# Opening the first four weight units of a two-block fp32 kernel block by block instead of one after the other

## The chip, the cores and the metric

One NeuronCore of a Trainium2 chip runs the whole program. The metric is the device time of one execution in microseconds, the median of several runs. Of the engines, PE (TensorE) multiplies, ACT (ScalarE) and DVE (VectorE) do the elementwise work, POOL (GpSimd) sets constants, and SP (SyncE) issues most transfers.

## The reference

Two transformer-like blocks on 256 tokens of width 1024, in fp32. Only the start of the first one matters here: the input is RMS-normalised and projected by one wide matrix.

```
def rmsnorm(x, g):
    xf = x.astype(jnp.float32)
    y = xf * lax.rsqrt(jnp.mean(xf * xf, axis=-1, keepdims=True) + EPS)
    return (y * g.astype(jnp.float32)).astype(x.dtype)
...
    proj = n @ w_in
    idx = np.cumsum(IN_SIZES)[:-1].tolist()
    z, xBC, dt_raw, q, k, v, r, a1, g_ssd, g_gla = jnp.split(proj, idx, axis=-1)
```

The kernel multiplies the weights with x times g and applies the factor of each token (the reciprocal root of its mean square) when the product is evacuated, so the matmuls need not wait for the norm, but every evacuation does.

## The kernel before

All big matrices come as a stream of weight **units**: 1024 inputs by 128 outputs, 512 KB, one row of 4 KB per partition. The inputs of a unit are eight **blocks** of 128. There are four slots (`RING`) in `raw`; unit u uses slot u mod 4 and PSUM bank u mod 4 of `acc`. Each fp32 operand is split into a high part, rounded to the fast matmul format, and the rest. ACT makes the high part of a unit (`split_hi`, `whi`, L1163), DVE the low part (`split_lo`, `wlo`, L1670). x times g is split the same way, block by block: `xh` on ACT (L1209), `xl` on DVE (L1677). A unit is three products per block (high by high, high by low, low by high), 24 matmuls of 128 by 256 tokens.

What sets the order is written out by hand, engine by engine, with semaphores between the engines. SP loads the next unit into a slot when `lo_ready` has counted the low part of the slot's last unit (L379 to L381). ACT may write `whi` of a slot when the slot's load has landed and PE is done with the unit that used it. PE may start a unit when its high part is there and its bank is evacuated.

The opening before: SP loads unit 0, both halves of x, unit 1, the small weights, units 2 and 3 (L367 to L373). ACT loads all the parameters (`par`), splits unit 0, the eight blocks of x, unit 1, squares x (L1212 to L1217, `sq`), splits units 2 and 3, and takes the root of the mean square (`rms`: `rt` for a row of all tokens, `rtt` for a column per token). PE runs 14 products of a constant tile as a warm-up (L713), then unit 0 block by block (L714), unit 1 (L716 to L722), the **small products** (24 matmuls with the 48 columns for dt and a gate, L592 to L600), the **statistics** (`stream_stats`, L567: the sum of the squares times 1/1024, once as a row, once per token), and from unit 2 on the ordinary `unit`. Behind unit 3 stand the **gates** (`gla_gates`, L602), which need the evacuated small products (`smt`, L1806). DVE adds the squares in four steps (L1763 to L1773), makes the reciprocals `rtok` (per token) and `rstd` (row), half of it `rstdh` (L1776), evacuates the small products, and then goes from unit to unit: evacuation (L1828), low part of the unit four further on, taps of a convolution.

Of the kernel before, what the change touches and what calls it, by code (L numbers as in the profile page):

```python
# [23 lines left out]
P = 128  # L24
F32 = mybir.dt.float32
# [9 lines left out]
KB = D // P  # L35
# [93 lines left out]
CHUNK_AT = {38: (0, 2), 40: (1, 3), 43: (4, 5)}  # L129
CONV_AT = [c + c // 2 + 1 for c in range(12)]  # L130
# [17 lines left out]
def blocks_kernel(nc, w, wsmall, wa2, par, xT, memT, metaT, out):  # L148
    with ExitStack() as ctx:
# [160 lines left out]
        def hidden(T):  # L310
# [12 lines left out]
        par_in, x_in, x2_in, meta_in, ws_in, wa_in, mem_in = [sem(n) for n in  # L323
            ("par_in", "x_in", "x2_in", "meta_in", "ws_in", "wa_in", "mem_in")]
# [148 lines left out]
        def _(pe):  # L473
# [236 lines left out]

            pe.wait_ge(consts, 2)
            for n in range(14):
                nc.tensor.matmul(mix[:, 2, 0:P], mean1024[:, :], mean1024[:, :], start=True, stop=True)  # L713
            unit("xbc", 0, 0, xh1, xl1, T1, ready=(xl_ready, 0))  # L714
            pe.wait_ge(hi_ready, 2)
            for k in range(KB):  # L716
                nc.tensor.matmul(acc[:, 1, 0:T1], whi[:, 1, k, :], xh1[:, k, 0:T1], start=k == 0, stop=False)
                nc.tensor.matmul(acc[:, 1, 0:T1], whi[:, 1, k, :], xl1[:, k, 0:T1], start=False, stop=False)
            pe.wait_ge(lo_ready, 2)
            for k in range(KB):  # L720
                last = nc.tensor.matmul(acc[:, 1, 0:T1], wlo[:, 1, k, :], xh1[:, k, 0:T1], start=False, stop=k == KB - 1)
            last.then_inc(unit_done, 1)  # L722
            small_products()
# [432 lines left out]
        def _(act):  # L1156
            def split_hi(base, units=0):

                j = base % 4
                act.wait_ge(landed[j], units * 4 + 16 * (base // 4 + 1))  # L1160
                if base >= RING:
# [1355 lines left out]
```

## Time and profile before

| | us |
|---|---|
| median of 3 runs | 1178.31 |
| lowest, highest | 1178.06, 1178.64 |
| span of the profiled execution | 1175.6 |
| PE busy in it | 1160.9 (99%) |
| DVE busy | 839.4 (71%) |
| ACT busy | 678.9 (58%) |

The span runs from the first to the last instruction of the profiled execution; some 2.7 us of the measured time lie around it. PE is busy in nine tenths or more of every slice but the first and the last. A busy PE in such a table is not a PE at its peak, since matmuls overlap; the times at which groups of matmuls begin say more than their busy time. In a timeline row the first number is the start in us from the start of the span, the second the duration of the group, "xN" the number of instructions, and the brackets tell how long the engine was idle before and what released it. A row with the engine "SPq" or "ACTq" is the issue of a transfer, and the DMA view gives the time from that start to the landing of all its data.

### The profile page before, as it was taken

What the parts mean: (1) busy time and instruction counts of PE and PEld (TensorE: products, weight loads), DVE (VectorE), ACT (ScalarE), POOL (GpSimd) and SP (SyncE); (2) the same over time, 40 slices, a digit from 0 to 9 for tenths busy, and PEclk for the clock granted to TensorE, in tenths of its full rate; (3) what the DMA queues carried; (4) which work ended last, traced back from release to release, by engine and by line L of the source; (5) the groups of instructions that cost most, each with busy time, mean ns of one, the idle gap of its engine ahead of it and who ended that gap; (6) DMA issues with size and microseconds to landing.
All of it is one profiled execution on the core that took longest, in us unless ns stands there. A gap on an engine that the chain in (4) does not pass through costs nothing.

```text
span 1175.6 us, 25261 instructions
## 1 busy us (share of the span) xinstructions
PE 1160.9 (99%) x9580; PEld 1140.0 (97%) x9580; DVE 839.4 (71%) x1249; ACT 678.9 (58%) x1029; POOL 46.6 (4%) x68
## 2 busy tenths in 40 slices
PE   8999999999999999999999999999999999999997
PEld 8999899999999999999999999999999999999997
DVE  7998767987856877776667748666545898776453
ACT  6755547656535666655556647656444777665442
POOL 2002311400000000000000000000000000000000
PEclk9999999999999999999999999999999999999998
DMA  6655434566553565656553426555565545666561
GB/s 226 190 174 175 128 107 143 183 225 187 164 159 126 164 201 190 191 185 189 180 152 113 123 73 209 176 171 190 190 180 170 160 144 165 212 182 193 182 194 54
DMA packets 56775, 197.51 MB, mean 168 GB/s; under 512 B 7153, under 2 KB 9457, under 8 KB 56577
## 3 DMA queue, kind: packets, MB, share of 16 engines
q1 hardware_dynamic: 54480, 193.68, 53.8%
q10 hardware_dynamic: 2224, 2.84, 0.8%
q8 instruction: 51, 0.84, 0.3%
q14 instruction: 20, 0.16, 0.0%
HBM read 195.45 MB, written 1.05 MB: 167 GB/s over the span
## 4 chain that ended last, share of the span: by engine, by line
PE 85%; DVE 9%; ACT 4%; issue 2%; DMA 0%; DVEq 0%; ACTq 0%
PE acc L482 14%; PE acc L483 14%; PE acc L488 14%; PE acc L476 11%; PE acc L478 11%; PE acc L477 11%; DVE wlo L1670 3%; ACT whi L1163 1%; PE acc L541 1%; PE acc L542 1%; PE acc L545 1%; PE mix L822 1%; PE mix L803 1%; DVE softp L2166 1%; DVE sp L2156 1%
## 5 line engine op out<-in xcount | busy, mean ns | idle before, releaser
L1670 DVE TENSOR_TENSOR wlo<-raw,whi 128x1024 fp32r<-128x1024 f32 x366 | 448.7, 1229 | 180.0 <-ACT whi L1163 179.8
L1163 ACT ACTIVATE whi<-raw 128x1024 fp32r<-128x1024 f32 x366 | 385.2, 1057 | 317.7 <-PE acc L488 158.5
L482 PE MATMUL acc<-xh,whi 128*128 128x256 f32 (+1 forms) x1448 | 358.2, 285 | 0.0
L483 PE MATMUL acc<-xl,whi 128*128 128x256 f32 (+1 forms) x1448 | 353.7, 282 | 0.0
L482 PEld LDWEIGHTS acc<-xh,whi 128*128 128x128 f32 x1448 | 271.8, 188 | 2.9 <-issue 2.3
L483 PEld LDWEIGHTS acc<-xl,whi 128*128 128x128 f32 x1448 | 272.7, 188 | 0.3
L488 PE MATMUL acc<-xh,wlo 128*128 128x256 f32 (+1 forms) x1448 | 202.2, 282 | 0.0
L478 PE MATMUL acc<-hh,wlo 128*128 128x256 f32 (+1 forms) x688 | 194.4, 283 | 0.0
L476 PE MATMUL acc<-hh,whi 128*128 128x256 f32 (+1 forms) x688 | 194.3, 282 | 0.0
L477 PE MATMUL acc<-hl,whi 128*128 128x256 f32 (+1 forms) x688 | 194.1, 282 | 0.0
L488 PEld LDWEIGHTS acc<-xh,wlo 128*128 128x128 f32 x1448 | 185.2, 188 | 0.0
L477 PEld LDWEIGHTS acc<-hl,whi 128*128 128x128 f32 x688 | 129.4, 188 | 0.0
L478 PEld LDWEIGHTS acc<-hh,wlo 128*128 128x128 f32 x688 | 129.3, 188 | 0.0
L476 PEld LDWEIGHTS acc<-hh,whi 128*128 128x128 f32 x688 | 129.3, 188 | 0.0
L476 PE MATMUL acc<-xh,whi 128*128 128x256 f32 (+1 forms) x272 | 77.3, 284 | 3.3 <-DVE xl L1677 3.3
L478 PE MATMUL acc<-xh,wlo 128*128 128x256 f32 (+1 forms) x272 | 76.6, 282 | 0.0
L477 PE MATMUL acc<-xl,whi 128*128 128x256 f32 (+1 forms) x272 | 76.6, 281 | 0.0
L476 PEld LDWEIGHTS acc<-xh,whi 128*128 128x128 f32 x272 | 51.1, 188 | 3.9 <-DVE wlo L1670 2.4
L482 PE MATMUL acc<-yh,whi 128*128 128x256 f32 (+1 forms) x224 | 54.3, 281 | 0.0
L483 PE MATMUL acc<-yl,whi 128*128 128x256 f32 (+1 forms) x224 | 54.3, 280 | 0.0
L477 PEld LDWEIGHTS acc<-xl,whi 128*128 128x128 f32 x272 | 51.2, 188 | 0.0
L478 PEld LDWEIGHTS acc<-xh,wlo 128*128 128x128 f32 x272 | 51.1, 188 | 0.0
(397 smaller groups left out, 1572.1 us busy)
## 6 DMA issues: line engine op xcount, KB each, us to landing
raw<-w SPq DMA_DIRECT2D x366, 512.0 KB, 3.7
hT<-xT SPq DMA_DIRECT2D x2, 512.0 KB, 6.3
mem<-memT ACTq DMA_DIRECT2D x1, 1024.0 KB, 7.3
rgw<-w ACTq DMA_DIRECT2D x2, 512.0 KB, 4.9
out<-hT SPq DMA_DIRECT2D x4, 128.0 KB, 2.5
out<-hT ACTq DMA_DIRECT2D x4, 128.0 KB, 2.8
xdt<-wsmall SPq DMA_DIRECT2D x1, 192.0 KB, 7.0
pr<-par ACTq DMA_DIRECT2D x1, 114.0 KB, 4.4
```

Source lines behind the costliest of these rows:

```text
L476: nc.tensor.matmul(dst, whi[:, slot, n, :], rh, start=first, stop=False)
L477: nc.tensor.matmul(dst, whi[:, slot, n, :], rl, start=False, stop=False)
L478: return nc.tensor.matmul(dst, wlo[:, slot, n, :], rh, start=False, stop=last)
L482: nc.tensor.matmul(dst, whi[:, slot, n, :], rh, start=first, stop=False)
L483: nc.tensor.matmul(dst, whi[:, slot, n, :], rl, start=False, stop=False)
L488: ins = nc.tensor.matmul(dst, wlo[:, slot, k, :], rh(k), start=False, stop=last and k == KB - 1)
L541: nc.tensor.matmul(dst, ah[:, k, at:at + n], whi[:, s:s + 2, k, :], start=k == 0, stop=False)
L542: nc.tensor.matmul(dst, al[:, k, at:at + n], whi[:, s:s + 2, k, :], start=False, stop=False)
L545: last = nc.tensor.matmul(dst, ah[:, k, at:at + n], wlo[:, s:s + 2, k, :], start=False, stop=k == KB - 1)
L803: last = nc.tensor.matmul(mix[:, h % 2, 256 * t:256 * t + 256], xqT[:, 2 * h + i, P * t:P * t + P], xkT[:, 2 * h + i, :], start=i == 0, st ...
L1163: act.activation(whi[:, j, :, :].rearrange("p k c -> p (k c)"), raw[:, j, :], ACT.Copy)\
L1670: dve.tensor_tensor(wlo[:, j, :, :].rearrange("p k c -> p (k c)"), raw[:, j, :], whi[:, j, :, :].rearrange("p k c -> p (k c)").bitcast(F32 ...
```

## The change

The first four units are opened together. Their weights come in five pieces by input block: blocks 0 and 1 of units 0 and 1, the same of units 2 and 3, then blocks 2-3, 4-5 and 6-7 of all four. x comes as block 0 (on ACT's queue), block 1, and then pairs, each ahead of the weights that meet it. ACT loads first only the eight parameter columns that scale x; the others go last on SP. For each piece ACT makes the high part and DVE the low part in one instruction, and PE does all products of a block for its units before it goes to the next block; only the last piece is done unit by unit. `hi_ready` and `lo_ready` jump by 4 at the last piece. The squares of blocks 0 to 3 stand behind the high part of blocks 4-5 on ACT, the others behind the last high part; the four adds stand behind the last low part on DVE. PE does the statistics before the small products, gates come behind unit 4, and the warm-up has 11 products. The row reciprocal comes first on DVE; the reciprocals per token, the halved factor and the evacuation of the small products stand behind the first evacuation and the low part of unit 4.

```diff
+LEFT = ((2, 4), (4, 6), (6, 8))
...
-            sp_.dma_start(raw[:, 0, :], w[0, :, :]).then_inc(landed[0], 16)
-            sp_.dma_start(hT[:, 0:4, META:T2], xT[:, 0:4, :]).then_inc(x_in, 16)
-            sp_.dma_start(hT[:, 4:8, META:T2], xT[:, 4:8, :]).then_inc(x2_in, 16)
-            sp_.dma_start(raw[:, 1, :], w[1, :, :]).then_inc(landed[1], 16)
+            for n in range(2):
+
+                sp_.dma_start(raw[:, 2 * n:2 * n + 2, 0:2 * P], w[2 * n:2 * n + 2, :, 0:2 * P].rearrange("j p c -> p j c"))\
+                    .then_inc(w_in[n], 16)
+                if n == 0:
+                    sp_.dma_start(hT[:, 1, META:T2], xT[:, 1, :]).then_inc(x_in[1], 16)
+            for n, (a, b) in enumerate(LEFT):
+
+                sp_.dma_start(hT[:, a:b, META:T2], xT[:, a:b, :]).then_inc(x_in[2 + n], 16)
+                sp_.dma_start(raw[:, :, P * a:P * b], w[0:RING, :, P * a:P * b].rearrange("j p c -> p j c"))\
+                    .then_inc(w_in[2 + n], 16)
             sp_.dma_start(wsr, wsmall).then_inc(ws_in, 16)
-            for j in range(2, RING):
-                sp_.dma_start(raw[:, j, :], w[j, :, :]).then_inc(landed[j], 16)
+            sp_.dma_start(pr[:, KB:NPAR], par[:, KB:NPAR]).then_inc(par_in, 16)
...
+            def open_block(units, k, n):
+
+
+                pe.wait_ge(xh_ready, k + 1)
+                pe.wait_ge(open_hi, n + 1)
+                for j in units:
+                    nc.tensor.matmul(acc[:, j, 0:T1], whi[:, j, k, :], xh1[:, k, 0:T1], start=k == 0, stop=False)
+                pe.wait_ge(xl_ready, k + 1)
+                for j in units:
+                    nc.tensor.matmul(acc[:, j, 0:T1], whi[:, j, k, :], xl1[:, k, 0:T1], start=False, stop=False)
+                pe.wait_ge(open_lo, n + 1)
+                for j in units:
+                    nc.tensor.matmul(acc[:, j, 0:T1], wlo[:, j, k, :], xh1[:, k, 0:T1], start=False, stop=False)
...
+            for n in range(2):
+                for k in range(2):
+                    open_block((2 * n, 2 * n + 1), k, n)
+            for n, (a, b) in enumerate(LEFT[:-1]):
+                for k in range(a, b):
+                    open_block(range(RING), k, n + 2)
+            pe.wait_ge(hi_ready, RING)
+            pe.wait_ge(xl_ready, KB)
+            for j in range(RING):
+                for k in range(*LEFT[-1]):
+                    high_products(acc[:, j, 0:T1], j, k, xh1[:, k, 0:T1], xl1[:, k, 0:T1], False)
+                if j == 0:
+                    pe.wait_ge(lo_ready, RING)
+                low_products(acc[:, j, 0:T1], j, range(*LEFT[-1]), lambda k: xh1[:, k, 0:T1], True)\
+                    .then_inc(unit_done, 1)
             pe.wait_ge(consts, 15)
             stream_stats("mix", T1, tiles1)
+            small_products()
...
-                    elif m > 1:
+                    elif m >= RING:
                         unit(phase, n, n % 4, xh1, xl1, T1)
-                    if m == 3:
+                    if m == 4:
                         gla_gates(0)
                         gla_gates(1)
...
+            act.dma_start(hT[:, 0, META:T2], xT[:, 0, :]).then_inc(x_in[0], 16)
+            act.dma_start(pr[:, 0:KB], par[:, 0:KB]).then_inc(mixw_in, 16)
...
+            for n in range(2):
+                act.wait_ge(x_in[n], 16)
+                block_hi(n)
+                open_hi_part(n, 2 * n, 2 * n + 2, 0, 2)
+            for n, (a, b) in enumerate(LEFT):
+                act.wait_ge(x_in[2 + n], 16)
+                for k in range(a, b):
+                    block_hi(k)
+                open_hi_part(n + 2, 0, RING, a, b)
+                if n == 1:
+                    for k in range(a):
+                        square(k, T1)
+            for k in range(4, KB):
+                square(k, T1)
...
-            inverse_rms("mix", T1, (P, P), halved=True)
-            dve.wait_ge(rstdh_ready, 1)
+            inverse_rms("mix", T1)
...
-                    if m == 0:
-
+                    if m == 1:
+
+                        for t in range(2):
+                            dve.reciprocal(rtok[:, t:t + 1], rtt[:, t:t + 1])
+                        dve.tensor_scalar(rstdh[:, 0:T1], rstd[:, 0:T1], 0.5, None, ALU.mult).then_inc(rstdh_ready, 1)
+                        dve.wait_ge(rstdh_ready, 1)
```

On ACT, the opening of the program before, from the first split of a unit (L1163; L1209 are blocks of x, L1167 squares, L1215 the small weights):

```order
L1163 ACTIVATE whi<-raw 128x1024 [waits landed0]
L1209 ACTIVATE xh<-hT,pr 128x256 [waits x_in,par_in]
L1209 ACTIVATE xh<-hT,pr 128x256 x3
L1209 ACTIVATE xh<-hT,pr 128x256 [waits x2_in]
L1209 ACTIVATE xh<-hT,pr 128x256 x3
L1163 ACTIVATE whi<-raw 128x1024 [waits landed1]
L1211 DMA bcn<-wa 16x512
L1167 ACTIVATE sq<-hT 128x256 x4
L1215 ACTIVATE wsh<-xdt 128x384 [waits ws_in]
L1167 ACTIVATE sq<-hT 128x256 x4
```

And now, the same engine from block 1 on (L1236 are blocks of x, L1232 high parts of a piece, L1196 squares):

```order
L1236 ACTIVATE xh<-hT,pr 128x256 [waits x_in1]
L1232 ACTIVATE whi<-raw 128x2x256 [waits w_in1]
L1236 ACTIVATE xh<-hT,pr 128x256 [waits x_in2]
L1236 ACTIVATE xh<-hT,pr 128x256
L1232 ACTIVATE whi<-raw 128x4x256 [waits w_in2]
L1236 ACTIVATE xh<-hT,pr 128x256 [waits x_in3]
L1236 ACTIVATE xh<-hT,pr 128x256
L1232 ACTIVATE whi<-raw 128x4x256 [waits w_in3]
L1196 ACTIVATE sq<-hT 128x256 x4
L1236 ACTIVATE xh<-hT,pr 128x256 [waits x_in4]
L1236 ACTIVATE xh<-hT,pr 128x256
L1232 ACTIVATE whi<-raw 128x4x256 [waits w_in4]
```

The blocks of x stand between the pieces, each with a landing of its own to wait for, and the first four squares ahead of the last piece.

On DVE before, from the low part of unit 1 to the first evacuation of a unit (L1763 to L1773 are the adds of squares, L1710 and L1711 the reciprocals, L1806 and L1809 the small products, L1828 the evacuation):

```order
L1763 TENSOR_TENSOR sq<-sq 128x2x256 [waits sq_ready]
L1765 TENSOR_TENSOR wsl<-xdt,wsh 128x384 [waits ws_ready]
L1769 TENSOR_TENSOR sq<-sq 128x2x256 [waits sq_ready]
L1771 TENSOR_TENSOR sq<-sq 128x2x256 [waits sum_ready]
L1773 TENSOR_TENSOR sq<-sq 128x256 [waits sum_ready]
L1670 TENSOR_TENSOR wlo<-raw,whi 128x1024 [waits hi_ready] x2
L1710 RECIPROCAL rtok<-rtt 128x1 [waits misc_free]
L1710 RECIPROCAL rtok<-rtt 128x1
L1711 RECIPROCAL rstd<-rt 128x256
L1715 TENSOR_SCALAR rstdh<-rstd 128x256 [waits rstd_ready]
L1806 TENSOR_TENSOR xdt<-mix,rstd 48x256 [waits small_done,consts,rstdh_ready]
L1809 TENSOR_SCALAR xdt<-xdt,pr 16x256 [waits small_read]
```

And now, from the low part of the last piece (L1799) on (L1812 to L1818 are the adds, L1751 the row reciprocal, L1880 the evacuation, L1854 the reciprocals per token):

```order
L1799 TENSOR_TENSOR wlo<-raw,whi 128x4x256 [waits hi_ready]
L1812 TENSOR_TENSOR sq<-sq 128x2x256 [waits sq_ready]
L1814 TENSOR_TENSOR sq<-sq 128x2x256 [waits sq_ready]
L1816 TENSOR_TENSOR sq<-sq 128x2x256 [waits sum_ready]
L1818 TENSOR_TENSOR sq<-sq 128x256 [waits sum_ready]
L1820 TENSOR_TENSOR wsl<-xdt,wsh 128x384 [waits ws_ready]
L1824 TENSOR_SCALAR small<-pr 128x60 [waits par_in]
L1751 RECIPROCAL rstd<-rt 128x256 [waits misc_free]
L1880 TENSOR_TENSOR convin<-acc,rstd 128x256 [waits unit_done,consts,rstd_ready]
L1710 TENSOR_TENSOR wlo<-raw,whi 128x1024 [waits hi_ready]
L1854 RECIPROCAL rtok<-rtt 128x1 x2
L1855 TENSOR_SCALAR rstdh<-rstd 128x256
```

The adds stood ahead of two low parts and stand behind all of them; the row reciprocal and the first evacuation have moved ahead of the token factors and the small products.

On PE now, the end of the opening (L492, L493 and L498 are the high and low products of the last piece, L569 and L573 the statistics, L606 the first of the small products):

```order
L493 MATMUL acc<-xl,whi 128x256
L498 MATMUL acc<-xh,wlo 128x256 x2
L569 MATMUL mix<-sq,mean 128x256 [waits sum_ready,consts]
L573 MATMUL mix<-mean,sq 128x1 x2
L606 MATMUL mix<-xh,wsh 48x256 [waits wsl_ready]
```

Before, the same place read:

```order
L721 MATMUL acc<-xh,wlo 128x256 [waits lo_ready]
L721 MATMUL acc<-xh,wlo 128x256 x7
L596 MATMUL mix<-xh,wsh 48x256 [waits wsl_ready]
L597 MATMUL mix<-xl,wsh 48x256
L598 MATMUL mix<-xh,wsl 48x256
```

The statistics came behind the small products and two units, and come now behind four units and ahead of the small products.

## Rows read from the trace of the kernel before

**Rows 1.** Stretch: length, busy PE, PEld, DVE, ACT, POOL, clock, DMA share, GB/s.
```profile
31.30:1175.60 1144.30, 1133.07 (x9372) 1113.02 (x9370) 816.70 (x1212) 657.61 (x991) 39.09 (x40) 1.00 0.55 167
```
**Rows 2.** Timeline of PE in the opening, firsts of each group.
```profile
8.30 0.36 PE L476 MATMUL acc<-xh,whi 128*128 128x256 f32 x1 [2.24 <-DVE xl L1677]
...
14.34 0.28 PE L596 MATMUL mix<-xh,wsh 128*48 128x256 f32 x1
...
17.14 0.60 PE L559 MATMUL mix<-sq,mean 128*128 128x256 f32 x2
...
17.94 0.36 PE L482 MATMUL acc<-xh,whi 128*128 128x256 f32 x1
...
23.71 1.99 PE L609 MATMUL mix<-xdt,bcn 16*128 16x256 f32 x8
25.63 0.38 PE L482 MATMUL acc<-xh,whi 128*128 128x256 f32 x1
...
28.54 0.28 PE L482 MATMUL acc<-xh,whi 128*128 128x256 f32 x1
...
31.34 0.28 PE L482 MATMUL acc<-xh,whi 128*128 128x256 f32 x1
```
**Rows 3.** Timeline of SP: the issues of unit 0 and x's two halves.
```profile
0.81 0.39 SPq L367 DMA_DIRECT2D raw<-w  x1
1.26 0.42 SPq L368 DMA_DIRECT2D hT<-xT  x1
1.73 0.50 SPq L369 DMA_DIRECT2D hT<-xT  x1
```
**Rows 4.** DMA view around each of these issues: KB, us to landing.
```profile
raw<-w SPq DMA_DIRECT2D x1, 512.0 KB, 4.2
...
hT<-xT SPq DMA_DIRECT2D x1, 512.0 KB, 5.8
...
hT<-xT SPq DMA_DIRECT2D x1, 512.0 KB, 6.8
```
**Rows 5.** Timeline of ACT in the opening.
```profile
7.12 2.90 ACT L1209 ACTIVATE xh<-hT,pr 128x256 fp32r<-128x256 f32 x7 [0.99 <-DMA hT<-xT]
...
9.93 0.49 ACT L1209 ACTIVATE xh<-hT,pr 128x256 fp32r<-128x256 f32 x1
10.33 1.05 ACT L1163 ACTIVATE whi<-raw 128x1024 fp32r<-128x1024 f32 x1
11.28 1.32 ACT L1167 ACTIVATE sq<-hT 128x256 f32<-128x256 f32 x4
```
**Rows 6.** Timeline of DVE in the opening.
```profile
11.41 1.23 DVE L1670 TENSOR_TENSOR wlo<-raw,whi 128x1024 fp32r<-128x1024 f32 x1 [0.46 <-ACT whi L1163]
12.64 0.69 DVE L1763 TENSOR_TENSOR sq<-sq 128x512 f32<-128x512 f32 x1
...
14.28 0.69 DVE L1769 TENSOR_TENSOR sq<-sq 128x512 f32<-128x512 f32 x1 [0.48 <-ACT sq L1167]
...
15.73 0.43 DVE L1773 TENSOR_TENSOR sq<-sq 128x256 f32<-128x256 f32 x1
```
**Rows 7.** Timeline of DVE behind the statistics.
```profile
18.66 0.23 DVE L1710 RECIPROCAL rtok<-rtt 128x1 f32<-128x1 f32 x2 [0.23 <-ACT rtt L1183]
18.80 1.74 DVE L1711 RECIPROCAL rstd<-rt 128x256 f32<-128x256 f32 x1
...
21.62 0.41 DVE L1828 TENSOR_TENSOR convin<-acc,rstd 128x256 f32<-128x256 f32 x1
...
27.86 1.22 DVE L1670 TENSOR_TENSOR wlo<-raw,whi 128x1024 fp32r<-128x1024 f32 x1 [1.32 <-ACT whi L1163]
...
36.77 0.40 DVE L1828 TENSOR_TENSOR convin<-acc,rstd 128x256 f32<-128x256 f32 x1
```
**Rows 8.** Timeline of PE: the first matmul of unit 9.
```profile
40.18 0.39 PE L482 MATMUL acc<-xh,whi 128*128 128x256 f32 x1
```
**Rows 9.** The page's table of DMA issues: loads of the weight stream.
```profile
raw<-w SPq DMA_DIRECT2D x366, 512.0 KB, 3.7
```

More of the change, by code:

```diff
@@ L322, in blocks_kernel @@
         consts = sem("consts")
-        par_in, x_in, x2_in, meta_in, ws_in, wa_in, mem_in = [sem(n) for n in
-            ("par_in", "x_in", "x2_in", "meta_in", "ws_in", "wa_in", "mem_in")]
+        par_in, mixw_in, meta_in, ws_in, wa_in, mem_in = [sem(n) for n in
+            ("par_in", "mixw_in", "meta_in", "ws_in", "wa_in", "mem_in")]
+        x_in = [sem(f"x_in{n}") for n in range(2 + len(LEFT))]
+        w_in = [sem(f"w_in{n}") for n in range(2 + len(LEFT))]
+        open_hi, open_lo = sem("open_hi"), sem("open_lo")
         xh_ready, xl_ready, sq_ready = sem("xh_ready"), sem("xl_ready"), sem("sq_ready")
@@ L711, in _ @@
             pe.wait_ge(consts, 2)
-            for n in range(14):
+            for n in range(11):
                 nc.tensor.matmul(mix[:, 2, 0:P], mean1024[:, :], mean1024[:, :], start=True, stop=True)
[L714 to L723, printed above, removed]
+            for n in range(2):
[4 more added lines that the diff above has]
+                    open_block(range(RING), k, n + 2)
@@ L1159, in split_hi @@
                 j = base % 4
-                act.wait_ge(landed[j], units * 4 + 16 * (base // 4 + 1))
-                if base >= RING:
-                    act.wait_ge(unit_done, units + (base - 3))
+                act.wait_ge(landed[j], units * 4 + 16 * (base // 4))
+                act.wait_ge(unit_done, units + (base - 3))
                 act.activation(whi[:, j, :, :].rearrange("p k c -> p (k c)"), raw[:, j, :], ACT.Copy)\
@@ L1754, in token_scaled, with open_lo_part @@
                         .then_inc(evacuated[m % 4 + t], 1)
[L1756 to L1761 removed]
+            def open_lo_part(n, j0, j1, a, b):
+                dve.wait_ge(*((hi_ready, RING) if b == KB else (open_hi, n + 1)))
+                dve.tensor_tensor(wlo[:, j0:j1, a:b, :].rearrange("p j k c -> p j (k c)"), raw[:, j0:j1, P * a:P * b],
+                                  whi[:, j0:j1, a:b, :].rearrange("p j k c -> p j (k c)").bitcast(F32), ALU.subtract)\
+                    .then_inc(*((lo_ready, RING) if b == KB else (open_lo, 1)))
+            dve.wait_ge(mixw_in, 16)
+            for n in range(2):
+                operand_lo("mix", n, T1, n)
+                open_lo_part(n, 2 * n, 2 * n + 2, 0, 2)
+            for n, (a, b) in enumerate(LEFT):
+                for k in range(a, b):
+                    operand_lo("mix", k, T1, k)
+                open_lo_part(n + 2, 0, RING, a, b)
             dve.wait_ge(sq_ready, 4)
             dve.tensor_tensor(sq[:, 2:4, 0:T1], sq[:, 0:2, 0:T1], sq[:, 2:4, 0:T1], ALU.add).then_inc(sum_ready, 1)
[L1764 to L1767 removed]
             dve.wait_ge(sq_ready, KB)
```

42 lines of the change are left out of this document (14 added, 28 removed).

## The prediction

> **What bounds the kernel now.** I read the table of stretches first: from 31.3 us on PE is busy 1133.07 of 1144.30 us [rows 1]. That part the change does not touch, and PE is never short of queued work there, so it can only move as a block. What can be won lies before. The PE timeline of the opening [rows 2] shows where: the first product starts at 8.30, after 2.24 us of idling; by 31.34 PE has done units 0 to 5 (24 matmuls each), the small products, the statistics and the gates. Each has its length there: a unit 2.80 (28.54 to 31.34), small products 2.80 (14.34 to 17.14), statistics 0.80 (17.14 to 17.94), gates 1.92 (23.71 to 25.63), a unit just behind the gates 2.91 (25.63 to 28.54). Both kernels start unit 6 with the same work behind them, so I compare that one moment: 31.34 now, against what the new opening gives. The DMA view with the SP timeline [rows 3, 4] tells when data lands, the ACT and DVE timelines [rows 5 to 7] what each step takes.
>
> **When the pieces land.** Before, three 512 KB loads stand in a row on SP: landing at 0.81 + 4.2 = 5.01 (w, 4 KB rows), 1.26 + 5.8 = 7.06 and 1.73 + 6.8 = 8.53 (x, written in 1 KB rows) [rows 3, 4]. So 512 KB in 1 KB rows took 2.05 us the first time and 1.47 the second. All new pieces are in 1 KB rows: per partition 256 columns of each unit, or one block of x. A load that had the engines to itself from the start would have begun to count at 5.01 - 1.47 = 3.54 (a little late, since the 5.01 was shared with the parameter load). In units of 512 KB, everything up to the weights of blocks 2-3 is 3.0, of blocks 4-5 4.5, of blocks 6-7 6.0 (x's quarter on the ACT queue counted in). I take the slow price for the first 1.75 (as far as it held before, 7.06) and the fast one behind: 3.54 + 3.59 + 1.25 x 1.47 = 8.97, then 11.17, then 13.38. The bounds are the fast price throughout (7.95, 10.16, 12.36) and the slow one throughout (9.69, 12.77, 15.84).
>
> Here a rule speaks against the change. Three loads queued one behind the other land 2.05 and 1.47 us apart, not each with the 4.2 us of a first one [rows 4]: a queue pays the fixed time once. The Trainium skill ("DMA: Bandwidth & Descriptors", section "Bandwidth") says to batch transfers to 1 MiB or more, because each carries about 2 us of fixed cost; the nine pieces on SP would by that come to an estimated 18 us of it alone. The rows say otherwise, and I go by them.
>
> **ACT and DVE behind the landings.** On ACT a full split follows the next instruction at a distance of 0.95 us (10.33 to 11.28), an x block at 0.40 (7.12 to 9.93 is seven), four squares take 1.32 [rows 5]. Parts 0 and 1 (blocks 0-1, two units at a time) are 24 matmuls, 2.8 us; their splits are half size, their data is in by 3.54 + 1.5 x 2.05 = 6.6, so PE has done them before 9.9 and then idles; the three warm-up products dropped and the smaller parameter load ahead of x cost nothing, since part 2 is what is waited for. Part 2: 8.97 + 0.95 + two x blocks 0.80 = 10.72, ahead of the landing of part 3 at 11.17. Part 3: 11.17 + 0.95 + four squares 1.32 + 0.80 = 14.24, by now later than the landing of part 4 (13.38). Part 4's split ends at 14.24 + 1.05 = 15.29. DVE's low part 1.23 [rows 6]: 16.55. PE does 4 matmuls of part 4, then waits for this and needs 20 more at 2.80 / 24: 18.88.
>
> The squares are the price of the new order. Before, the sum was ready at 15.73 + 0.43 = 16.16 [rows 6] and nobody waited, for PE only came to it at 17.14 [rows 2]. Now the four adds stand behind DVE's last low part: 0.69 for the first, then 16.16 - 14.28 = 1.88 for the other three: 16.55 + 0.69 + 1.88 = 19.12 [rows 6]. The last four squares end at about 16.5 and are not the later ones. So PE is ready at 18.88 and the sum at 19.12: the sum ends last, by 0.2.
>
> **From the sum to unit 6.** Statistics 0.80: 19.92. Small products now stand behind them and hide 2.80 of what evacuation needs. Before, the row reciprocal began 18.80 - 17.94 = 0.86 behind the statistics, after the two token factors that began at 18.66 [rows 7]; these 0.14 are moved away: 0.72 + 1.74 + the first evacuation 0.41 + joint = 2.90. So unit 4 starts 2.90 behind the statistics, 0.1 later than small products alone would let it. Its weights are no bar: slot 0 is free at 16.55, a load in the full loop takes 3.7 us [rows 9], 20.3, then one split. Then unit 4 2.80, gates 1.92, unit 5 2.91, joints 0.1: 19.92 + 2.90 + 7.73 = 30.5. Against 31.34 that is a gain of 0.8 us. What was moved behind the first evacuation (token factors, halved factor, dt inputs: about 0.14 + 21.62 - 20.54 = 1.2 us of DVE [rows 7]) comes before the gates need it.
>
> The profiled execution was 1175.6 us long, the median of the runs 1178.31; the 2.7 around it stay. So **1178.31 - 0.8 = 1177.5**. With the fast price throughout, part 3 lands at 10.16 and all behind it comes 1.0 earlier: 1176.5. With the slow one throughout part 4 starts at 15.84 instead of 14.24: 1.6 later, 1179.1.
>
> **Rivals.**
> 1. Strided pieces load more slowly than x did, and the kernel ends slower. For it: before, weights are read as whole 4 KB rows, now as quarters of rows, four units side by side, which no row of before shows; the DMA engines are the thing waited for. Against: x is written in the same 1 KB rows at 1.47. It decides from 2.0 us per 512 KB on (no gain left) and passes 0.2% at 2.3 us: 3.54 + 6 x 2.31 = 17.4 for part 4. At twice the fast price, 2.94, part 4 lands at 21.2, 6.9 later: 1184.4. A fixed time paid by every piece would show in the same place, as landings that drift further apart than their bytes, and is held in the same chance.
> 2. DVE becomes the bound behind the opening. Between its first evacuation at 21.62 and its sixth at 36.77 it has 1.32 us of idling, for ACT's split at 27.86 [rows 7], and gets 1.2 us more to do. Counted from the end of the statistics the sixth evacuation ends at 2.90 + 15.15 + 1.2 = 19.2 and PE wants that bank for unit 9 at 10.6 + 8.84 (31.34 to 40.18 [rows 2, 8]) = 19.4. Before, it had 3 us to spare, now 0.2. A slip of half a microsecond eats part of the gain: 1178.0.
> 3. The clock falls. PE idles about a microsecond before part 2, having been only partly busy since its warm-up. Before, it idled 2.24 us and a later matmul still took the 0.28 it takes in full flow [rows 2]; the granted clock of the stretches is 1.00, which is 2.4 GHz [rows 1]. The Trainium skill ("TensorE: Matmul & The Clock Gate", section "Why this matters for your kernels") warns that idle gaps put the clock back to half; by the row a gap as long as 2.24 did not. If it fell for one part, 24 matmuls would take 5.6 instead of 2.8: 1179.5 with the slack taken off.
> 4. The pieces land faster than any row shows. Over 0.2% needs part 3 at 9.6, or 1.35 us per 512 KB: 1175.9.
>
> **How the numbers follow.** Forecast, with rates between the two x rows, 0.73: 1176.5 to 1179.1, likeliest 1177.5. Slow pieces 0.12, two thirds of that beyond 0.2%. DVE 0.07, clock 0.03, faster landing 0.05. To hold 8 in 10 I take 1176.2 to 1179.5. 0.2% is 2.36 us, about what a measurement can tell from no change; the forecast lies well inside: faster 0.05, same 0.86, slower 0.09.
>
> **What would show it.** In the profile after: first product of parts 0-1 at about 6, an idle stretch of PE before part 2 that ends at a split waiting for a landing near 9; ACT without idling between the split of part 3 and that of part 4; the statistics' matmul waiting for DVE's last add at about 19; first evacuation 2.9 behind the statistics; unit 6 at 30.5. Wrong would be: weights of blocks 6-7 landing after 15, statistics waiting for PE rather than for the sum, matmuls of twice the usual length, or a wait of units 8 to 10 for evacuations.

## The result

The changed kernel takes 1180.04 us (median of 11 runs, 1179.19 to 1180.79), the kernel before in runs on the same chip 1177.44 (11 runs, 1177.04 to 1178.78): a ratio of 1.0021, 95% interval 1.0013 to 1.0029. The change costs 2.6 us where a gain of 0.8 was forecast, and the time lies outside the range. The 1178.31 that the forecast starts from is the median of three of the runs before; all eleven give 0.9 less, so the time misses its forecast by 2.5 us and the change by 3.4. The profiled execution spans 1178.2 us, against 1175.6.

### The profile page after: what moved, and what is told of

Read it like the earlier page. It is cut to its first block, busy times and chain, and to the rows that moved or that the text cites. A ratio compares the mean times of both kernels' runs of the same rounds, so it can differ in the third digit from the quotient of the medians.

```text
span 1178.2 us, 25269 instructions
## 1 busy us (share of the span) xinstructions
PE 1162.1 (99%) x9574; PEld 1139.7 (97%) x9574; DVE 839.4 (71%) x1250; ACT 678.8 (58%) x1030; POOL 46.3 (4%) x68
## 4 chain that ended last, share of the span: by engine, by line
PE 81%; DVE 12%; ACT 5%; issue 2%; DMA 1%; SPq 0%; DVEq 0%; ACTq 0%
PE acc L492 14%; PE acc L498 13%; PE acc L493 13%; PE acc L486 11%; PE acc L488 10%; PE acc L487 10%; DVE wlo L1710 5%; ACT whi L1192 1%; DVE xc L1843 1%; PE acc L551 1%; PE acc L555 1%; PE acc L552 1%; DMA raw<-w 1%; PE mix L852 1%; PE mix L833 1%
## 5 line engine op out<-in xcount | busy, mean ns | idle before, releaser
L1710 DVE TENSOR_TENSOR wlo<-raw,whi 128x1024 fp32r<-128x1024 f32 x362 | 443.9, 1229 | 178.6 <-ACT whi L1192 178.3
L1192 ACT ACTIVATE whi<-raw 128x1024 fp32r<-128x1024 f32 x362 | 381.0, 1057 | 309.0 <-PE acc L498 155.1
L492 PE MATMUL acc<-xh,whi 128*128 128x256 f32 (+1 forms) x1440 | 356.3, 285 | 0.2 <-DVE convin L1880 0.2
L493 PE MATMUL acc<-xl,whi 128*128 128x256 f32 (+1 forms) x1440 | 352.0, 282 | 0.0
L492 PEld LDWEIGHTS acc<-xh,whi 128*128 128x128 f32 x1440 | 270.6, 188 | 3.3 <-issue 2.7
L493 PEld LDWEIGHTS acc<-xl,whi 128*128 128x128 f32 x1440 | 270.9, 188 | 0.3
L498 PE MATMUL acc<-xh,wlo 128*128 128x256 f32 (+1 forms) x1440 | 201.6, 282 | 0.0
L498 PEld LDWEIGHTS acc<-xh,wlo 128*128 128x128 f32 x1440 | 184.2, 188 | 0.1
L486 PE MATMUL acc<-xh,whi 128*128 128x256 f32 (+1 forms) x264 | 74.7, 283 | 1.1 <-DVE xl L1717 1.1
L488 PE MATMUL acc<-xh,wlo 128*128 128x256 f32 (+1 forms) x264 | 74.4, 282 | 0.0
L492 PE MATMUL acc<-yh,whi 128*128 128x256 f32 (+1 forms) x224 | 54.3, 281 | 0.0
L493 PE MATMUL acc<-yl,whi 128*128 128x256 f32 (+1 forms) x224 | 54.2, 280 | 0.0
L487 PEld LDWEIGHTS acc<-xl,whi 128*128 128x128 f32 x264 | 49.6, 188 | 0.0
L488 PEld LDWEIGHTS acc<-xh,wlo 128*128 128x128 f32 x264 | 49.6, 188 | 0.0
```

The lines of the kernel that those rows point to most:

```text
L486: nc.tensor.matmul(dst, whi[:, slot, n, :], rh, start=first, stop=False)
L487: nc.tensor.matmul(dst, whi[:, slot, n, :], rl, start=False, stop=False)
L488: return nc.tensor.matmul(dst, wlo[:, slot, n, :], rh, start=False, stop=last)
L492: nc.tensor.matmul(dst, whi[:, slot, n, :], rh, start=first, stop=False)
L493: nc.tensor.matmul(dst, whi[:, slot, n, :], rl, start=False, stop=False)
L498: ins = nc.tensor.matmul(dst, wlo[:, slot, k, :], rh(k), start=False, stop=last and k == KB - 1)
```

## The profile after, beside that of before

The opening itself ends only 0.4 us later. PE in the opening of the changed kernel (start, duration, group, idle time before it and its releaser), to be read against [rows 2]:

```profile
6.64 0.48 PE L727 MATMUL acc<-xh,whi 128*128 128x256 f32 x2 [0.38 <-ACT whi L1232]
...
10.98 0.71 PE L727 MATMUL acc<-xh,whi 128*128 128x256 f32 x4 [0.85 <-ACT whi L1232]
...
19.94 0.67 PE L569 MATMUL mix<-sq,mean 128*128 128x256 f32 x2
...
23.95 0.36 PE L492 MATMUL acc<-xh,whi 128*128 128x256 f32 x1 [0.16 <-DVE convin L1880]
...
26.92 1.99 PE L619 MATMUL mix<-xdt,bcn 16*128 16x256 f32 x8
28.84 0.38 PE L492 MATMUL acc<-xh,whi 128*128 128x256 f32 x1
...
31.74 0.28 PE L492 MATMUL acc<-xh,whi 128*128 128x256 f32 x1
```

Unit 6 starts at 31.74 where it was 31.34 [rows 2]. The statistics start at 19.94 where it was 17.14 [rows 2]: 2.8 later, for PE now does four units ahead of them instead of two and the small products.

The loss is behind the opening. Stretches of the changed kernel (length, then busy PE, PEld, DVE, ACT, POOL, clock, DMA share, GB/s):

```profile
31.70:82.00 50.30, 50.30 (x431) 50.14 (x431) 49.16 (x91) 30.75 (x44) 0.00 (x0) 1.00 0.64 189
82.00:94.00 12.00, 10.28 (x82) 9.56 (x80) 9.74 (x12) 8.80 (x13) 0.00 (x0) 1.00 0.52 161
```

The same stretches of the kernel before, 0.4 earlier:

```profile
31.30:81.60 50.30, 50.30 (x431) 50.14 (x430) 49.14 (x90) 31.73 (x45) 0.00 (x0) 1.00 0.62 186
81.60:93.60 12.00, 12.00 (x101) 11.70 (x100) 8.86 (x11) 7.64 (x13) 0.00 (x0) 1.00 0.55 176
```

For 50 us the two run alike, PE busy throughout. Then PE loses 1.72 us of busy time within 12. (Its starts slip by more there, 2.35 us, because the modelled end of a matmul covers part of each wait; starts are the better measure.) What PE waited for between 31 and 100 us in the changed kernel (the same view of the kernel before has no row):

```profile
PE mix L633 <- DVE xc L1945: 0.7, 1, 0.7
PE mix L641 <- DVE xdt L1971: 0.6, 1, 0.6
PE acc L551 <- ACT vt L1346: 0.4, 1, 0.4
```

Three handovers, one behind the other: the last output of the convolution, which the product in `cb` reads, the evacuation of a pair of value units on ACT, which a later value unit needs for its bank, and a bank of transposes (`x_by_token`) that DVE has to empty. None is in the part that the diff touches. All three come from DVE and ACT, and both are late from the statistics on. DVE in the changed kernel, against [rows 6, 7]:

```profile
17.32 0.69 DVE L1812 TENSOR_TENSOR sq<-sq 128x512 f32<-128x512 f32 x1
...
19.37 0.43 DVE L1818 TENSOR_TENSOR sq<-sq 128x256 f32<-128x256 f32 x1
...
21.59 1.75 DVE L1751 RECIPROCAL rstd<-rt 128x256 f32<-128x256 f32 x1 [1.22 <-ACT rtt L1212]
23.38 0.42 DVE L1880 TENSOR_TENSOR convin<-acc,rstd 128x256 f32<-128x256 f32 x1
...
30.76 1.23 DVE L1710 TENSOR_TENSOR wlo<-raw,whi 128x1024 fp32r<-128x1024 f32 x1 [1.29 <-ACT whi L1192]
45.28 1.23 DVE L1710 TENSOR_TENSOR wlo<-raw,whi 128x1024 fp32r<-128x1024 f32 x1 [0.32 <-ACT whi L1192]
57.80 1.23 DVE L1710 TENSOR_TENSOR wlo<-raw,whi 128x1024 fp32r<-128x1024 f32 x1 [0.61 <-ACT whi L1192]
...
82.02 1.22 DVE L1937 TENSOR_TENSOR etmp<-bcn 128x1024 f32<-128x1024 f32 x1
87.81 1.23 DVE L1710 TENSOR_TENSOR wlo<-raw,whi 128x1024 fp32r<-128x1024 f32 x1 [1.96 <-ACT whi L1192]
```

And the matching four instructions of the kernel before (the first idle stretch, 1.32, is in [rows 7]):

```profile
42.39 1.22 DVE L1670 TENSOR_TENSOR wlo<-raw,whi 128x1024 fp32r<-128x1024 f32 x1 [0.31 <-ACT whi L1163]
54.91 1.23 DVE L1670 TENSOR_TENSOR wlo<-raw,whi 128x1024 fp32r<-128x1024 f32 x1 [0.61 <-ACT whi L1163]
79.14 1.23 DVE L1885 TENSOR_TENSOR etmp<-bcn 128x1024 f32<-128x1024 f32 x1
84.93 1.23 DVE L1670 TENSOR_TENSOR wlo<-raw,whi 128x1024 fp32r<-128x1024 f32 x1 [1.96 <-ACT whi L1163]
```

This is what gives the case away. The row reciprocal is 2.79 later (21.59 against 18.80). The first evacuation is only 1.76 later (23.38 against 21.62), since the token factors and what belongs to them moved behind it; with them done, the low part at 30.76 is 2.90 later, the operation near 80 us 2.88, the low part near 85 us 2.88: from there on DVE is late by a constant amount. It has idle stretches, 4.2 us of them, but they are of the same length in both kernels (1.29 and 1.32, 0.32 and 0.31, 0.61 twice, 1.96 twice), so they absorb nothing. DVE waits there for ACT's high part, and ACT in turn was held up by work that DVE releases to it (the bias of the convolution, the steps of the gates). Ahead of the low part at 42.39, for example, ACT is busy without a break from 39.86 on, when DVE's evacuation releases a bias to it; in the changed kernel that starts at 42.74, again 2.88 later. The two engines wait for each other in a fixed pattern that hangs on the row reciprocal, and that pattern moves as one piece.

How much of this PE feels depends on how long before PE's arrival the pattern used to deliver. The lateness of PE (start in the changed kernel less that in the kernel before) goes 0.40 up to 82 us, 1.28 at `cb`, 2.00 at the value unit, 2.75 at the transposes near 91 us, and then stays. So the first handover had 1.6 us to spare (2.88 - 1.28), the second 0.9, the third 0.14 (the starts before rounding are 2.89 and 2.75 late).

The third lead can be read directly, from the last evacuation by DVE and the transposes that need its bank. Before:

```profile
89.28 1.28 DVE L1919 TENSOR_TENSOR xdt<-mix,ctok 128x512 f32<-128x512 f32 x2
90.31 1.04 PE L631 MATMUL mix<-ident,xc 128*128 128x128 f32 x8
```

And changed:

```profile
92.16 1.28 DVE L1971 TENSOR_TENSOR xdt<-mix,ctok 128x512 f32<-128x512 f32 x2
...
93.50 0.66 PE L641 MATMUL mix<-ident,xc 128*128 128x128 f32 x4 [0.60 <-DVE xdt L1971]
```

In the changed kernel DVE ends at 93.44 and PE goes on 0.06 later, with the second four transposes. Before, DVE ended at 90.56 and the fifth of the eight transposes, which follow each other at 0.11 us, began at 90.75: 0.19 later, of which 0.06 is the handover. That leaves the 0.13 to 0.14.

## The experiments

**The theory.** DVE and ACT form a chain from the statistics on, with 0.14 us to spare at its last handover to PE, 91 us into the program. The change delays the statistics, so the kernel is later by the chain's lateness less that. **The rival.** The pieces themselves cost: their landings, their splits, the loads of the ring that follow them.

**1. The delay without the change.** Idle adds on DVE in the kernel before, ahead of the reciprocals, five or three of them:

```diff
+            dve.tensor_tensor(t4[:, 0:2, 0:T1], hT[:, 0:2, META:T2], hT[:, 4:6, META:T2], ALU.add)
...
             inverse_rms("mix", T1, (P, P), halved=True)
             dve.wait_ge(rstdh_ready, 1)
```

> The kernel before, with five idle adds of two blocks each (results unused) on DVE ahead of the reciprocals behind the statistics. At 0.62 us each they take 3.1 us, of which 0.23 fills an idle stretch: the reciprocal of the row starts at about 21.7 instead of 18.80, as late as it is in the changed kernel (21.59). Landings, squares, statistics and the order of units stay as before. Theory (the DVE and ACT chain that starts at the statistics is what ends late): units 4 and 5 wait a few tenths at most, PE runs on without a wait to about 82 us, then waits for the conv taps, the token factors' evacuation and the inputs of the scan, 0.4 to 0.7 us each, and the kernel ends 2.0 to 2.8 us later. Rival (what costs is the landing of the pieces and what PE loses in its own opening): not more than the 0.5 us that units 4 and 5 may wait, 0 to 0.5.

> The kernel before with three such adds instead of five: 1.9 us, of which 0.23 was idle, so the row reciprocal starts 1.65 us later, at about 20.4. Theory: if the chain has next to no slack, 1.2 to 1.6 us later; if it has a slack of 0.9 us or more, which the forecast's kind of reading supposed, 0.8 or less, and the first waits of PE come later than 82 us. Rival (landings, PE's own opening): 0.

With five: 1180.47 us against 1177.37, ratio 1.0025 (1.0015 to 1.0035), a little more than expected. With three: 1178.52, ratio 1.0011 (1.0002 to 1.0020), or 1.15 us, just below the theory's 1.2 to 1.6. PE's waits with five adds, between 80 and 95 us, are the same three:

```profile
83.49 0.67 PE L623 MATMUL mix<-xc 128*128 128x256 f32 x2 [0.51 <-DVE xc L1898]
...
86.30 0.36 PE L541 MATMUL acc<-whi,xh 128*128 128x256 f32 x1 [0.40 <-ACT vt L1306]
...
93.25 0.66 PE L631 MATMUL mix<-ident,xc 128*128 128x128 f32 x4 [0.59 <-DVE xdt L1924]
```

The kernel before, with its own loads, splits and order, loses all that the change loses, only because DVE is late at that place. The row reciprocal starts at 21.46 and 20.34, that is 2.66 and 1.54 late, and PE is 2.50 and 1.38 late at 91 us. Each time 0.16 less, whatever the dose. With three adds PE does not wait at the first handover at all, only at the second (0.3) and third (0.6): a lateness of 1.5 lies within the first one's 1.6 and beyond the 0.9 of the second. The gates waited 0.4 us in the stronger case, which is within what was expected and hides behind the later waits.

**2. The chain made short.** The taps of the convolution on 16 of 256 columns, in both kernels:

```diff
-                dve.scalar_tensor_tensor(out=xc[:, c, :], in0=convin[:, c, tap:tap + T1],
+                dve.scalar_tensor_tensor(out=xc[:, c, 0:16], in0=convin[:, c, tap:tap + 16],
```

> The changed kernel with the taps of the convolution done on 16 of 256 columns (the other columns are left out), which takes most of 0.47 us off each of 36 taps on DVE up to 82 us, some 13 us. Theory: the lateness of 2.9 us behind the statistics is worked off, the waits of PE between 82 and 94 us are gone, and against the kernel before with the same cut what stays is PE's own opening, +0.4 us (0 to 0.8). Rival (the time is lost elsewhere: slower loads behind the opening, the clock, the landings): the difference stays at 2.6.

> The kernel before with the same cut (taps on 16 of 256 columns, the others left out). It is there to be compared with the changed kernel so cut. Theory: PE waits for nothing between 31 and 100 us in the kernel before, so it gains less than 0.5 us there from the cut itself; later stages with the same taps may gain on their own account, in both alike.

1177.61 us (ratio to the kernel before 1.0004, 0.9995 to 1.0013) and 1177.35 (1.0001, 0.9992 to 1.0010). The difference of 2.6 has become 0.26. The whole changed opening is still in the first of the two, with its pieces, its landings and its late statistics (row reciprocal at 21.17). DVE is 2.4 late there at first, works that off in the idle stretches that the lighter taps leave, and starts the operation near 80 us at 77.14, against 77.11 in the other. PE's waits are gone from both traces. And the lighter kernel before gains nothing: DVE's work there is hidden as long as it is on time, which is why no share of busy time warned of it.

**3. The statistics put back, the pieces kept.** Squares between the pieces on ACT, the adds ahead of the last low part on DVE, statistics and small products ahead of the last piece on PE, reciprocals as before:

```diff
+            pe.wait_ge(consts, 15)
+            stream_stats("mix", T1, tiles1)
+            small_products()
             pe.wait_ge(hi_ready, RING)
...
+                if n == 0:
+                    dve.wait_ge(sq_ready, 4)
+                    add_pairs(2, 0, 2)
+                if n == 2:
+                    dve.wait_ge(sq_ready, KB)
+                    add_pairs(6, 4, 6)
...
                 open_lo_part(n + 2, 0, RING, a, b)
```

> The changed kernel, still opening four units together, but with the statistics as early as the squares allow: squares on ACT between the pieces, the adds on DVE ahead of the last low part, statistics and small products on PE ahead of the last piece, and the order of the reciprocals as before (all three, the small products' evacuation, then the first unit). Theory: the sum is ready at about 17.6 and the row reciprocal starts at about 18.9 instead of 21.59, so the chain is as early as in the kernel before; PE reaches unit 6 at 31.3 to 31.9 and waits for nothing at 82 to 94 us; against the kernel before -0.2 to +0.6 us, some 2 us faster than the changed kernel. Rival (the pieces, strided, are what costs): as slow as the changed kernel, +2.6.

1178.66 us against 1177.64, ratio 1.0007 (0.9999 to 1.0016). The row reciprocal starts at 18.60, a little ahead of the 18.9 expected, and PE is ahead at unit 6. But the end is 1.0 later than the kernel before, not -0.2 to 0.6: better than the rival's 2.6, and a miss. (The interval just reaches no change; the trace has PE 1.13 late at 91 us.) The trace says where. ACT in this kernel:

```profile
22.16 1.06 ACT L1192 ACTIVATE whi<-raw 128x1024 fp32r<-128x1024 f32 x1 [3.73 <-DMA raw<-w]
```

The loads of the units from 4 on, on its SP:

```profile
18.44 8.40 SPq L390 DMA_DIRECT2D raw<-w  x6
```

And its DVE:

```profile
21.52 0.41 DVE L1882 TENSOR_TENSOR convin<-acc,rstd 128x256 f32<-128x256 f32 x1
23.25 1.23 DVE L1709 TENSOR_TENSOR wlo<-raw,whi 128x1024 fp32r<-128x1024 f32 x1 [1.32 <-ACT whi L1192]
```

The same low part in the kernel before:

```profile
21.95 1.20 DVE L1670 TENSOR_TENSOR wlo<-raw,whi 128x1024 fp32r<-128x1024 f32 x1
```

The chain is 0.10 early at the first evacuation (21.52 against 21.62 [rows 7]) and 1.30 late at the next instruction, the low part of unit 4 (23.25 against 21.95): its weights have not landed. The last low part frees all four slots at once, at 18.3, and only then, at 18.44, does the load of unit 4 start. Before, slot 0 was free when unit 0 was split, and the load started at 7.90. The next experiment tests this.

**4. Other work in that gap.** The same kernel, with the evacuations of the four opened units and the taps of one channel block ahead of unit 4's low part, and the small products behind the last piece:

```diff
+                    if m == 0:
+                        for k in range(RING):
+                            dve.wait_ge(unit_done, k + 1)
+                            dve.tensor_tensor(convin[:, k, 3:3 + T1], acc[:, k, 0:T1], rstd[:, 0:T1], ALU.mult)\
+                                .then_inc(evacuated[k], 1)
+                        for tap in (2, 1, 0):
+                            conv_tap(0, tap)
```

> The changed kernel with the statistics first (as in the run after_stats), and further: small products behind the last piece on PE; on DVE the evacuations of all four opened units and the three taps of channel block 0 stand ahead of the low part of unit 4, and on ACT the conv bias of unit 0 ahead of unit 4's high part, so that DVE has work while unit 4's weights are still loading (after_stats had an idle stretch of 1.32 us there, behind which its chain was 1.30 late). Theory: the chain is then 0 to 0.4 us late against the kernel before, PE's lateness at 91 us is this less about 0.17, and the time is within 0.4 us of the kernel before, about 1 us less than after_stats and 2.3 less than the changed kernel. Rival (a part of the loss is in the pieces or in the loads that follow them): no better than after_stats, +1.0.

1177.58 us against 1177.34, ratio 1.0002 (0.9993 to 1.0012): not measurably slower than the kernel before. The idle stretch ahead of unit 4's low part is gone, but a new one came two units on (DVE again):

```profile
23.40 1.22 DVE L1712 TENSOR_TENSOR wlo<-raw,whi 128x1024 fp32r<-128x1024 f32 x1
...
29.07 1.23 DVE L1712 TENSOR_TENSOR wlo<-raw,whi 128x1024 fp32r<-128x1024 f32 x1 [2.23 <-ACT whi L1192]
```

ACT does the high part of unit 6 behind the steps of the gates, which now come later since the small products do. So the chain ends 1.00 late near 80 us where 0 to 0.4 was expected, and PE is 0.86 late at 91 us. The time came out inside what was expected, the chain did not. PE's lateness is still the chain's less 0.14, and of the three handovers only the last one makes it wait.

**5. The order alone, without the pieces.** In the kernel before, units 0 to 3 whole as they were, then statistics, then small products:

```diff
-            small_products()
-            pe.wait_ge(consts, 15)
-            stream_stats("mix", T1, tiles1)
...
+                    if m == 3:
+                        pe.wait_ge(consts, 15)
+                        stream_stats("mix", T1, tiles1)
+                        small_products()
+                    if m == 4:
                         gla_gates(0)
```

With it goes the edit of experiment 6 below, since the small products are later.

> The kernel before, with its own loads, splits and low parts (unit 0, unit 1, then 2 and 3, each whole), and of the change only the order behind them: PE does units 0 to 3, then the statistics, then the small products; gates behind unit 4; row reciprocal first on DVE, token factors and small products' evacuation at the second unit. PE reaches the statistics at 14.34 + 2 x 2.80 = 19.94, as in the changed kernel, and unit 6 at about 31.3, so its own opening loses nothing. Theory (DVE and ACT's chain from the statistics on sets the end, with a slack of about 0.2 us): the chain is 2.8 late, PE waits at 82, 85 and 91 us, and the kernel ends 2.4 to 2.8 us later than before. Rival (the pieces, their landing and their splits are what costs): 0 to 0.3.

1181.20 us against 1177.34, ratio 1.0037 (1.0024 to 1.0051): 3.9 us later than before where 2.4 to 2.8 was expected, and about 1.2 later than the changed kernel. PE waits for unit 2's high part, which the small products used to cover, and starts that unit at 15.29 instead of 14.34; the unit itself takes 0.35 longer than the 2.80 of a unit. So the statistics start at 21.26:

```profile
15.29 0.39 PE L482 MATMUL acc<-xh,whi 128*128 128x256 f32 x1 [0.72 <-ACT whi L1164]
...
21.26 0.59 PE L559 MATMUL mix<-sq,mean 128*128 128x256 f32 x2
```

The forecast of the delay was 1.3 too small; the relation holds, 4.07 late in the chain near 80 us and 3.93 on PE. So the opening in pieces is worth about 1.2 us of what this order costs: the pieces are not the culprit, they pay part of the bill.

**6. The reciprocal alone.** The last edit of the change on the kernel before, PE's order untouched:

```diff
-            inverse_rms("mix", T1, (P, P), halved=True)
-            dve.wait_ge(rstdh_ready, 1)
+            inverse_rms("mix", T1)
...
-                    if m == 0:
+                    if m == 1:
+                        for t in range(2):
+                            dve.reciprocal(rtok[:, t:t + 1], rtt[:, t:t + 1])
+                        dve.tensor_scalar(rstdh[:, 0:T1], rstd[:, 0:T1], 0.5, None, ALU.mult).then_inc(rstdh_ready, 1)
```

> The kernel before with one edit of the change alone: row reciprocal first, token factors, halved factor and the small products' evacuation behind the first evacuation of a unit and its low part. Theory: nothing lies on the chain that this shortens, since the same instructions stand on DVE in another order: -0.2 to +0.3 us, with the gates as the only place where PE could wait (the evacuated small products come about 2 us later, at 23.6, and the gates begin at 23.71). Rival (this edit is what brings the loss): +1 or more.

1177.44 us against 1177.64, ratio 0.9998 (0.9990 to 1.0007): no loss of 1 us or more, and nothing that can be told from no change. Its profiled execution, 1178.2 us of span, met something else, which the last section tells.

**7. POOL and the landings.** POOL's constants set only behind the sixth block of x, in either kernel:

```diff
                 pool.memset(tile[:, :], value).then_inc(consts, 1)
+                if tile is mean1024:
+                    pool.wait_ge(xh_ready, 6)
```

> The changed kernel with POOL's constants (all but the first two) set only behind the sixth block of x, so that POOL writes nothing while the opening's loads land. The loads had a slow spell at 5.4 to 6.9 us (229 to 243 GB/s, against some 340 around it). Theory: POOL's writes are not what slows them, landings within 0.2 us of those of the changed kernel and the time the same. Rival (they are): blocks 2-3 of x land about 1 us earlier, everything up to the statistics moves with them, and the kernel ends 0.7 to 1.0 us sooner.

> The kernel before with the same delay of POOL's constants. Theory: no change of the landings (weights of unit 0 at 5.0, x at 7.1 and 8.5) nor of the time. Rival: the first half of x lands about 0.5 us earlier and PE starts as much earlier, 0.3 to 0.6 us sooner at the end.

1180.59 (ratio 1.0021, 1.0013 to 1.0030) and 1177.51 (0.9994, 0.9986 to 1.0003): no change of either time. The slow spell of the loads is there with POOL idle, though from 5 to 6 us they are faster (277 against 244 GB/s). Stretches of the changed kernel (POOL's busy time is the fifth of the engines', GB/s the last column):

```profile
5.00:6.00 1.00, 1.00 (x6) 0.97 (x5) 0.00 (x0) 0.53 (x2) 0.93 (x4) 1.00 0.84 244
6.00:7.00 1.00, 0.62 (x5) 0.39 (x4) 0.90 (x2) 1.00 (x3) 0.95 (x2) 1.00 0.89 229
7.00:8.00 1.00, 0.84 (x8) 0.64 (x7) 1.00 (x3) 0.42 (x1) 0.98 (x2) 1.00 1.03 339
```

And of the changed kernel with POOL held back:

```profile
5.00:6.00 1.00, 0.35 (x4) 0.16 (x2) 0.00 (x0) 0.41 (x1) 0.00 (x0) 1.00 0.96 277
6.00:7.00 1.00, 0.24 (x2) 0.27 (x3) 0.78 (x2) 1.00 (x4) 0.00 (x0) 1.00 0.90 221
7.00:8.00 1.00, 1.00 (x9) 0.87 (x9) 1.00 (x3) 0.57 (x3) 0.00 (x0) 1.00 1.02 356
```

ACT got blocks 2-3 of x at 7.96 instead of 8.35, and part 2 of the weights at 9.47 instead of 9.78: between the two expectations. The time cannot decide here, since POOL's work, moved under the sum of squares, made the first three adds 0.44 us longer in all (the last section shows it), PE waited 0.3 us for the sum, and the row reciprocal came at 21.73, even 0.14 later. Single executions differ by some tenths, so this part is not settled. In the kernel before the landings stayed (ACT's first weights at 5.10, first x at 7.16, against 5.08 and 7.12). What slows the loads between 5 and 7 us stays open.

**All together**, lateness in us against the profiled execution of before: the chain at DVE's operation near 80 us (79.14 before), PE at the second four transposes near 91 us (90.75 before). The numbers are from starts before rounding.

| kernel | chain | PE at 91 us | difference | median less that of before |
|---|---|---|---|---|
| changed | 2.89 | 2.75 | 0.14 | 2.6 |
| changed, POOL later | 3.03 | 2.89 | 0.14 | 3.0 |
| changed, statistics first | 1.28 | 1.13 | 0.15 | 1.0 |
| the same, gap filled | 1.00 | 0.86 | 0.14 | 0.2 |
| before, five adds | 2.64 | 2.50 | 0.14 | 3.1 |
| before, three adds | 1.52 | 1.38 | 0.14 | 1.2 |
| before, late statistics | 4.07 | 3.93 | 0.14 | 3.9 |

Seven kernels with different openings, one difference: each time DVE, not PE's own work, sets when PE goes on at 91 us, and the way from the one operation to the other takes the two engines equally long. The medians follow within 0.6 us, which is about what single executions scatter by.

No version here is measurably faster than the kernel before.

## Why the prediction was wrong

**The landings.** ACT in the changed kernel:

```profile
8.35 0.91 ACT L1236 ACTIVATE xh<-hT,pr 128x256 fp32r<-128x256 f32 x2 [0.93 <-DMA hT<-xT]
9.78 1.06 ACT L1232 ACTIVATE whi<-raw 128x1024 fp32r<-128x1024 f32 x1 [0.52 <-DMA raw<-w]
...
12.05 1.06 ACT L1232 ACTIVATE whi<-raw 128x1024 fp32r<-128x1024 f32 x1 [0.41 <-DMA raw<-w]
```

Part 2 was in ACT's hands at 9.78, forecast 8.97, and just past the slow bound of 9.69. Behind it the fast price was right: part 3 at 12.05, 2.27 later, where 2.20 was forecast. So rival 1 held for the first pieces only: counted from the prediction's 3.54, the first 1.5 MB came at 2.08 us per 512 KB (its bound of 2.0 should read 1.9, where 3.54 + 6 x 1.92 uses up the gain of 0.8). Behind the slow spell at 5 to 7 us the weights of one piece and the x ahead of it land as their bytes do, and rival 4, faster landings, did not occur.

The fixed cost of about 2 us for each transfer, which the prediction names, is stated by the Trainium skill ("DMA: Bandwidth & Descriptors") in its section "Anatomy of one DMA — SWDGE (gpsimd) path", as a fit to transfers that POOL issues. Two loads would by that carry an estimated 4 us; the 2.27 us for part 3 and the x ahead of it show no such cost for loads that SP queues one behind the other.

**ACT, DVE and the sum.** The order forecast for ACT is the one in the trace; the statistics began at 19.94, forecast 19.12: 0.8 later, as much as part 2 landed late, for PE works without a break from 10.98 on. The sum was ready at 19.37 + 0.43 = 19.80, so PE, not the sum, came last, by 0.14. From there to unit 6 it took 11.8 us, forecast 11.4: unit 4 started 4.0 behind the start of the statistics (forecast 0.80 + 2.90) and took 2.97. So unit 6 came at 31.74 instead of 30.5: a gain of 0.8 turned into a loss of 0.4, of which two thirds are the landing. By itself that would have stayed inside the range.

**The step that failed** is the first one: "PE is never short of queued work there, so it can only move as a block", and with it the comparison at unit 6 alone. It was true of the kernel before, where PE waited for nothing between 31 and 100 us. But that PE does not wait does not say by how much. At 91 us DVE was 0.14 us ahead of PE, and the same forecast moved DVE: by its own terms the first evacuation would begin at 19.92 + 2.90 - 0.41 = 22.4 instead of 21.62, 0.8 later, with another 1.2 us of work put behind it. So DVE would be 2.0 late where PE had 0.14 to spare: the kernel 1.86 us later instead of 0.8 earlier, on the forecast's own landings. With the 0.8 of the landing on top it is an estimated 2.7; PE was 2.75 late at 91 us, and the median rose by 2.6. The rows for that were in the trace of the kernel before; they were followed up to unit 9 and no further.

**Rival 2** had the mechanism, DVE as the bound, with a chance of 0.07 and a wrong place. It counted to the bank of unit 9, where PE indeed did not wait, and priced a slip at half a microsecond without working that out. The 1.32 us of DVE's idling that it names took up nothing, since ACT's part that ends it moved along.

**Rival 3**, the clock, did not occur in the changed kernel: granted 1.00 from 4 to 14 us, with idle stretches of 0.38 and 0.85 us of PE. **The reciprocal's edit**, valued at 0.14, gained nothing that can be measured: experiment 6 rules out a large effect (its interval is -1.2 to +0.8 us) and cannot resolve 0.14. The same instructions stand on DVE, in another order, and the chain needs them all.

## What to carry over

Before moving work into an opening, follow each engine that serves the bottleneck, not only the bottleneck, to the place where its lead is smallest, and read the lead there: an engine that never waits may be 0.1 us from waiting. Idle time on such an engine is slack only if what ends it does not itself depend on that engine. A constant lateness from row to row, with idle stretches of unchanged length, tells that a pattern of two engines moves as one.

## What the hardware showed that was not expected

**The clock can fall in the opening.** The run with the reciprocal's edit shares the opening of the kernel before up to the statistics. In the profiled execution of the reciprocal's run PE idled 2.03 us behind the warm-up, and these stretches show the granted clock in the last column but two:

```profile
8.00:9.00 1.00, 0.47 (x2) 0.50 (x3) 1.00 (x3) 1.00 (x4) 0.11 (x1) 0.81 1.02 399
9.00:10.00 1.00, 1.00 (x6) 1.00 (x6) 1.00 (x4) 1.00 (x4) 0.00 (x0) 0.50 1.07 408
```

The clock stays at 0.50, the 1.2 GHz level, up to 12 us, and matmuls follow each other at 0.21 us instead of 0.12 meanwhile; PE comes to the statistics 1.46 late. The prediction concluded from one trace that an idle stretch of 2.24 us leaves the clock alone. The clock stayed at 1.00 in that execution, and behind 2.43 us in the run with three adds; here it fell behind a shorter stretch. So one trace was too little for that conclusion, though what set this execution apart was not tested. The Trainium skill ("TensorE: Matmul & The Clock Gate", section "Why this matters for your kernels") warns that idle gaps put the clock back; the traces bear that out in one execution of these three, and not behind the longest stretch.

**DVE and POOL slow each other.** With POOL's constants moved under the sum of squares the first three adds took 0.78, 0.89 and 0.84 us, where each took 0.69 in the changed kernel:

```profile
17.02 0.78 DVE L1814 TENSOR_TENSOR sq<-sq 128x512 f32<-128x512 f32 x1
17.72 0.89 DVE L1816 TENSOR_TENSOR sq<-sq 128x512 f32<-128x512 f32 x1
18.64 0.84 DVE L1818 TENSOR_TENSOR sq<-sq 128x512 f32<-128x512 f32 x1
```

POOL of the same kernel at that time:

```profile
16.53 0.73 POOL L435 TENSOR_SCALAR_AFFINE_SELECT tri<-tri 128x128 f32<-128x128 f32 x1
17.22 1.76 POOL L438 TENSOR_SCALAR_AFFINE_SELECT cmask<-cmask 128x256 bf16<-128x256 bf16 x2
```

The first of these in the changed kernel, where DVE was idle from 5 to 6 us:

```profile
5.56 0.29 POOL L433 TENSOR_SCALAR_AFFINE_SELECT tri<-tri 128x128 f32<-128x128 f32 x1
```

The Trainium skill ("SBUF — State Buffer", section "Who interferes with whom") says that a DVE instruction with two inputs in SBUF contends with a POOL instruction that reads SBUF. The trace agrees: beside each other the adds took 0.09 to 0.20 us longer, and the select of `tri` 0.73 us instead of 0.29, though durations on POOL are rough.
